# Sums of weight blocks in the gate and product buffers, and both seven-product fours of a chunk one behind the other

## What is computed

```python
D_FF = 5632
def swiglu(x, w_gate, w_up, w_down):
    return (jax.nn.silu(x @ w_gate) * (x @ w_up)) @ w_down

x = x + 0.5 * swiglu(rmsnorm(x, ffn1_norm[i]), ffn1_w_gate[i], ffn1_w_up[i], ffn1_w_down[i])
x = x + hybrid_mixer(...)
x = x + 0.5 * swiglu(rmsnorm(x, ffn2_norm[i]), ffn2_w_gate[i], ffn2_w_up[i], ffn2_w_down[i])
```

## Time and profile before

| | us |
|---|---|
| median of 3 runs | 2666.16 (2665.12 to 2667.31) |
| the profiled execution | 2666.6 |
| its span, first to last instruction | 2664.8 |
| PE busy | 2597.6 (97%) |
| VectorE busy | 1769.4 (66%) |
| ScalarE busy | 1259.4 (47%) |
| GpSimd busy | 202.7 (8%) |

### The profile page before, as it was taken

How to read it: one execution, slowest core, us unless ns; L and a number is a source line. 1 busy time by engine, 2 the same in 40 slices (tenths; PEclk the granted TensorE clock), 3 DMA queues, 4 the chain that set the end, 5 groups by cost and what they waited for, 6 DMA issues and landing times.

```text
span 2664.8 us, 32709 instructions
## 1 busy us (share of the span) xinstructions
PE 2597.6 (97%) x11549; PEld 2132.5 (80%) x11549; DVE 1769.4 (66%) x2077; ACT 1259.4 (47%) x1464; POOL 202.7 (8%) x345
## 2 busy tenths in 40 slices
PE   9999999999999999999999999999999899999998
PEld 8888888777777778888888888888877777778887
DVE  7766766887778765556555665555677787776554
ACT  5544554554444444444444554444454444444333
POOL 0121100000000000001100410000000000000000
PEclk9999999999999999999999999999999999999999
DMA  7887775565665676668765676666765556657554
GB/s 220 258 252 234 216 231 170 195 207 189 219 206 197 202 231 213 207 211 259 244 210 175 215 226 210 208 209 208 220 199 189 197 199 207 200 190 259 194 193 158
DMA packets 280067, 561.53 MB, mean 211 GB/s; under 512 B 22826, under 2 KB 25784, under 8 KB 279720
## 3 DMA queue, kind: packets, MB, share of 16 engines
q1 hardware_dynamic: 257120, 489.61, 56.4%
q0 software_dynamic: 22208, 70.19, 8.5%
q10 hardware_dynamic: 648, 0.52, 0.1%
HBM read 526.02 MB, written 34.22 MB: 210 GB/s over the span
## 4 chain that ended last, share of the span: by engine, by line
PE 54%; issue 22%; DMA 11%; DVE 9%; ACT 2%; POOL 1%; DVEq 0%; ACTq 0%; SPq 0%; POOLq 0%
PE acc L635 45%; DMA raw<-in_ffn_w_up 7%; DVE wlo L1637 6%; PE acc L747 2%; PE acc L754 2%; PE acc L750 2%; DMA raw<-in_ffn_w_gate 2%; ACT whi L1164 2%; DMA qk<-turn_dram 1%; DMA turn_dram<-turned_s 1%; DVE raw L1667 1%; PE s_ps L854 1%; DVE raw L1657 1%; PE tr L770 1%; DMA turn_dram<-mix_turned 1%
## 5 line engine op out<-in xcount | busy, mean ns | idle before, releaser
L1637 DVE TENSOR_TENSOR wlo<-raw,whi 128x1024 fp32r<-128x1024 f32 (+2 forms) x1009 | 1191.9, 1200 | 763.4 <-ACT whi L1164 756.2
L1164 ACT ACTIVATE whi<-raw 128x1024 fp32r<-128x1024 f32 (+2 forms) x1009 | 1037.4, 1038 | 1113.9 <-PE acc L635 641.2
L635 PE MATMUL acc<-whi,act_hi 128*128 128x512 f32 (+1 forms) x1280 | 348.5, 393 | 0.1
L635 PE MATMUL acc<-whi,act_lo 128*128 128x512 f32 (+1 forms) x1280 | 341.2, 388 | 0.0
L635 PE MATMUL acc<-wlo,act_hi 128*128 128x512 f32 (+1 forms) x1280 | 341.1, 388 | 0.0
L747 PE MATMUL acc<-whi,act_hi 128*128 128x512 f32 x1040 | 294.1, 395 | 44.4 <-ACT whi L1164 44.4
L754 PE MATMUL acc<-wlo,act_hi 128*128 128x512 f32 x1040 | 293.2, 395 | 3.3 <-DVE wlo L1637 3.2
L750 PE MATMUL acc<-whi,act_lo 128*128 128x512 f32 x1040 | 292.3, 394 | 0.0
L635 PEld LDWEIGHTS acc<-whi,act_lo 128*128 128x128 f32 x1280 | 239.2, 188 | 50.4 <-DVEq L1756 0.4
L635 PEld LDWEIGHTS acc<-wlo,act_hi 128*128 128x128 f32 x1280 | 239.3, 188 | 50.1 <-DVE wlo L1637 0.4
L747 PEld LDWEIGHTS acc<-whi,act_hi 128*128 128x128 f32 x1040 | 192.8, 188 | 99.3 <-ACT whi L1164 60.7
(11 more groups left out here) (331 smaller groups left out, 2131.4 us busy)
## 6 DMA issues: line engine op xcount, KB each, us to landing
raw<-in_w_in SPq DMA_DIRECT2D x280, 512.0 KB, 4.4
raw<-in_ffn_w_gate SPq DMA_DIRECT2D x176, 512.0 KB, 5.2
raw<-in_ffn_w_up SPq DMA_DIRECT2D x176, 512.0 KB, 4.6
raw<-in_ffn_w_down SPq DMA_DIRECT2D x176, 512.0 KB, 4.6
raw<-in_w_out SPq DMA_DIRECT2D x64, 512.0 KB, 4.8
turn_dram<-h_turned POOLq DMA_DIRECT2D x25, 512.0 KB, 2.9
h_back<-turn_dram POOLq DMA_DIRECT2D x100, 128.0 KB, 2.9
raw<-in_w_sg_out SPq DMA_DIRECT2D x24, 512.0 KB, 4.2
```

What stands on the lines that cost most here:

```text
L635: return nc.tensor.matmul(pair[:, half, 0:width], left[:, j * TILES + t, half * P:(half + 1) * P], right[:, (first_group + j) % RING, t, 0 ...
L1164: nc.scalar.activation(whi[:, slot, tiles, 0:width], raw[:, slot, tiles, 0:width], ACT.Copy).then_inc(hi_ready, 1)
L1637: nc.vector.tensor_tensor(wlo[:, slot, tiles, 0:width], raw[:, slot, tiles, 0:width], whi[:, slot, tiles, 0:width].bitcast(F32), ALU.subtr ...
```

## The change

The block sums are written to `g_sb` (outer) and `h_sb` (inner) in place of `raw`, and ScalarE and VectorE split those two groups from there. They announce themselves on a semaphore `sums_made` in place of `raw_in`. A place of `raw` now belongs to the n-th load (`load_index`), not to the n-th group, so all four places hold loads: 16 loads in a chunk of 20 groups. The load n waits for the split of the group that load n - 4 belongs to (`place_of_load`). The order of a chunk is now: 0 to 3 left 2 to 5, 4 to 7 the first four, 8 to 11 the second four, 12 and 13 left 6 and 7, 14 to 19 right 2 to 7. `fours_out` moves with `LAST_FOUR` from position 13 to 11; the adding of the gate's bank becomes `left_out` and stands at `LEFT_DONE`, position 13; silu stays at position 15.

```diff
--- before.py
+++ after.py
@@ -105,17 +105,40 @@
     return [(part, k) for part in FOUR_PARTS]
-CHUNK_ORDER = ([("left", k) for k in range(2, 6)] + four(0) + [("left", 6), ("left", 7)] + four(1)
+CHUNK_ORDER = ([("left", k) for k in range(2, 6)] + four(0) + four(1) + [("left", 6), ("left", 7)]
                + [("right", k) for k in range(2, G_D)])
 CHUNK_GROUPS = len(CHUNK_ORDER)
 SUMS_PER_CHUNK = FOURS + 4 + 1
 LAST_FOUR = max(o for o, (kind, _) in enumerate(CHUNK_ORDER) if kind == "inner")
...
+LEFT_DONE = max(o for o, (kind, _) in enumerate(CHUNK_ORDER) if kind in ("left", "inner"))
 FFN_GROUPS = 2 * G_D + (FF_CHUNKS - 1) * CHUNK_GROUPS + CHUNKS * KF // TILES
 MIXER_GROUPS = 15 * G_D + CHUNKS * (2 * G_D + 2 + 6) + CHUNKS * G_D
 FFN_AT = [FIRST_GROUPS + CHUNKS * G_D]
 FFN_AT.append(FFN_AT[0] + FFN_GROUPS + MIXER_GROUPS)
 ALL_GROUPS = FFN_AT[1] + FFN_GROUPS
-KIND = {at + 2 * G_D + o: kind for at in FFN_AT for o, (kind, _) in enumerate(CHUNK_ORDER)}
+FOUR_AT = [o for o, (kind, _) in enumerate(CHUNK_ORDER) if kind == "four_left"]
+LOOPS = [at + 2 * G_D for at in FFN_AT]
+KIND = {at + o: kind for at in LOOPS for o, (kind, _) in enumerate(CHUNK_ORDER)}
+CHUNK_LOADS = sum(kind not in ("outer", "inner") for kind, _ in CHUNK_ORDER)
+def load_index(m):
+    n = m
+    for at in LOOPS:
+        if m >= at:
+            chunks, o = divmod(min(m - at, (FF_CHUNKS - 1) * CHUNK_GROUPS), CHUNK_GROUPS)
+            n -= chunks * (CHUNK_GROUPS - CHUNK_LOADS)
+            n -= sum(kind in ("outer", "inner") for kind, _ in CHUNK_ORDER[:o])
+    return n
+def place_of_load(n, below):
+    m = below - 1
+    while KIND.get(m) in ("outer", "inner") or load_index(m) != n:
+        m -= 1
+    return m
@@ -179,7 +202,7 @@
 def outer_tiles(m):
-    left, right = m % RING, (m + 1) % RING
+    left, right = load_index(m) % RING, load_index(m + 1) % RING
@@ -427,10 +451,12 @@
             at = Place()
             def load(w, k, col, width=W, extra=None):
-                slot = at.n["group"] % RING
-                if at.n["group"] >= RING:
-                    sp.wait_ge(lo_ready, at.target("group", 1 - RING))
+                n = load_index(at.n["group"])
+                slot = n % RING
+                if n >= RING:
+                    before = place_of_load(n - RING, at.n["group"])
+                    sp.wait_ge(lo_ready, at.target("group", before + 1 - at.n["group"]))
                 rows = w[k * TILES * P:(k + 1) * TILES * P, :].rearrange("(t p) n -> p t n", p=P)
                 main = width - (HEADS if extra is not None else 0)
                 cols = slice(col, col + main) if isinstance(col, int) else bass.ds(col, main)
@@ -1153,15 +1179,22 @@
                     return
                 width = LAT2 if LAT2_FIRST <= m < LAT2_END else W
                 slot = m % RING
-                target = raw_target(m)
-                if at.turn is not None:
-                    target = target + at.turn * (16 * at.adds["group"] // RING)
-                act.wait_ge(raw_in[slot], target)
+                if KIND.get(m) in ("outer", "inner"):
+                    at.n["made"] += 1
+                    act.wait_ge(sums_made, at.target("made"))
+                    source = g_sb if KIND[m] == "outer" else h_sb
+                else:
+                    place = load_index(m)
+                    target = raw_target(place)
+                    if at.turn is not None:
+                        target = target + at.turn * (16 * at.adds.get("load", at.adds["group"]) // RING)
+                    act.wait_ge(raw_in[place % RING], target)
+                    source = raw[:, place % RING, :, :]
                 if m >= RING:
                     act.wait_ge(group_used, at.target("group", n + 1 - RING))
                 tiles = slice(1, 2) if KIND.get(m) == "four_right" else slice(0, TILES)
-                nc.scalar.activation(whi[:, slot, tiles, 0:width], raw[:, slot, tiles, 0:width],
+                nc.scalar.activation(whi[:, slot, tiles, 0:width], source[:, tiles, 0:width],
                                      ACT.Copy).then_inc(hi_ready, 1)
             def groups(count, last_split=True):
@@ -1480,14 +1514,15 @@
                         act.wait_ge(four_summed, 1 if first_one else 2)
                         nc.scalar.activation(four_hi, four_raw, ACT.Copy).then_inc(four_rounded, 1)
                 at.n["turn"] = EX_FFN1 if first_one else EX_FFN2
-                for i in at.loop(act, FF_CHUNKS - 1, dict(group=CHUNK_GROUPS, unit=2, chunk=1, turn=1, paired=1)):
+                for i in at.loop(act, FF_CHUNKS - 1, dict(group=CHUNK_GROUPS, unit=2, chunk=1, turn=1, paired=1,
+                                                          load=CHUNK_LOADS, made=2 * FOURS)):
                     for j in paired():
                         if j == 5:
                             turned_hi(h_hi, i * 4, h_back[:])
                         if j == LAST_FOUR:
                             unit_ready()
                             nc.scalar.activation(g_sb[:, 0, :], q1[:], ACT.Copy).then_inc(q1_copied, 1)
-                        if j == LAST_FOUR + 2:
+                        if j == LEFT_DONE + 2:
                             act.wait_ge(acc_free[at.n["unit"] % 2], at.target("unit", 0, 2, 2) + 2)
                             for half in range(HALVES):
                                 last = nc.scalar.activation(g_sb[:, half, :], g_sb[:, half, :], ACT.Silu,
@@ -1634,7 +1669,7 @@
                     outer_sums(m + 1)
                 tiles = slice(1, 2) if KIND.get(m) == "four_right" else slice(0, TILES)
                 dve.wait_ge(hi_ready, at.target("group", n + 1))
-                nc.vector.tensor_tensor(wlo[:, slot, tiles, 0:width], raw[:, slot, tiles, 0:width],
+                nc.vector.tensor_tensor(wlo[:, slot, tiles, 0:width], split_source(m)[:, tiles, 0:width],
                                         whi[:, slot, tiles, 0:width].bitcast(F32), ALU.subtract).then_inc(lo_ready, 1)
                 if sums_next:
                     inner_sums(m + 1)
@@ -1643,32 +1678,38 @@
             def raw_filled(m):
-                target = raw_target(m)
+                n = load_index(m)
+                target = raw_target(n)
                 if at.turn is not None:
-                    target = target + at.turn * (16 * at.adds["group"] // RING)
-                dve.wait_ge(raw_in[m % RING], target)
+                    target = target + at.turn * (16 * at.adds.get("load", at.adds["group"]) // RING)
+                dve.wait_ge(raw_in[n % RING], target)
             def outer_sums(m):
                 raw_filled(m)
                 raw_filled(m + 1)
                 dve.wait_ge(lo_ready, at.target("group", m - 1 - at.n["group"]))
-                slot = (m + 2) % RING
-                nc.vector.tensor_tensor(raw[:, slot, :, :], raw_blocks[:, outer_tiles(m)[0], :],
-                                        raw[:, (m + 1) % RING, 0, :].unsqueeze(1).to_broadcast([P, TILES, W]),
-                                        ALU.add).then_inc(raw_in[slot], 16)
+                nc.vector.tensor_tensor(g_sb[:], raw_blocks[:, outer_tiles(m)[0], :],
+                                        raw[:, load_index(m + 1) % RING, 0, :].unsqueeze(1).to_broadcast([P, TILES, W]),
+                                        ALU.add).then_inc(sums_made, 1)
+                at.n["made"] += 1
             def inner_sums(m):
-                raw_filled(m + 2)
+                dve.wait_ge(turned, at.target("turn", at.n["turn"] in (EX_FFN1, EX_FFN2)))
+                dve.wait_ge(sums_made, at.target("made"))
                 dve.wait_ge(lo_ready, at.target("group", m - at.n["group"]))
-                slot = (m + 3) % RING
-                at.n["sums"] += 1
-                nc.vector.tensor_tensor(raw[:, slot, 0, :], raw[:, (m + 2) % RING, outer_tiles(m)[1], :],
-                                        raw[:, (m + 1) % RING, 1, :], ALU.add).then_inc(sum_step, 1)
-                dve.wait_ge(sum_step, at.target("sums"))
-                nc.vector.tensor_tensor(raw[:, slot, 1, :], raw[:, slot, 0, :], raw[:, m % RING, 1, :],
-                                        ALU.add).then_inc(raw_in[slot], 16)
+                sum_settled(nc.vector.tensor_tensor(h_sb[:, 0, :], g_sb[:, outer_tiles(m)[1], :],
+                                                    raw[:, load_index(m + 1) % RING, 1, :], ALU.add))
+                nc.vector.tensor_tensor(h_sb[:, 1, :], h_sb[:, 0, :], raw[:, load_index(m) % RING, 1, :],
+                                        ALU.add).then_inc(sums_made, 1)
+                at.n["made"] += 1
+            def split_source(m):
+                if KIND.get(m) in ("outer", "inner"):
+                    return g_sb if KIND[m] == "outer" else h_sb
+                return raw[:, load_index(m) % RING, :, :]
             def paired():
                 for j in range(CHUNK_GROUPS):
@@ -1712,6 +1754,10 @@
```

(11 more changed lines are left out.)

## The result

The changed kernel takes 2596.14 us (median of 4 runs, 2593.17 to 2597.23) against 2665.81 us before (2665.12 to 2667.31): a ratio of 0.9736, 95% interval 0.9719 to 0.9753, 69.7 us less. The forecast was 2620 with a range from 2602 to 2646.

What follows compares the result with a forecast made beforehand. PE bounds the kernel; only its stops in 20 feed-forward chunks can be won, 4.0 us each. With 1.7 us left a chunk, 20 x (4.0 - 1.7) = 46 us, so 2666 - 46 = 2620 us, range 2602 to 2646.

Steps and rivals of the forecast that it cites:

- What bounds the kernel: PE is nearly always busy; only its stops in feed-forward chunks can be won, 4.0 us each, 80 us in 20.
- The loss behind the fours: PE's stops in front of groups 8 and 14, about 2.4 us a chunk, go as four loads lead instead of two.
- Gating starts at 0.2 us: VectorE's gating starts 0.2 us behind a chunk's group 0, not 1.98, as its run behind the products is broken up.
- The walk: Step-by-step VectorE start times through both fours, from group 0's start, giving PE's stops at groups 8 to 10.
- S: Start of the second four's outer sums: 11.1 us, or group 9's load landing if later; 11.75 taken with a 5.1 us load.
- The formula for PE's loss: PE loses S + 5.1 - 16.55 at group 8 if positive, about 1.0 at group 9, plus restarts: 1.7 us a chunk.
- the lower end of the working: With group 9's load landing at 10.8 us, PE loses 0.7 + 0.3 = 1.0 us a chunk; time 2606 us.
- Rival 1: VectorE enters the fours as late as now, gating near 1.98 us: loss 2.8 to 3.8 us, 2642 to 2662 us; chance 0.25.
- rival 4: Loads limited by DMA engines, so the ring leads by no more and plain groups still wait: 2660 to 2667 us; chance 0.06.
- Rival 2: No load is late and VectorE's last splits overlap better: loss 1.0 us or less, 2600 to 2606 us; chance 0.10.
- Rival 3: Slower: second outer sums await group 9's load ahead of split 7, each microsecond stopping PE for one; 2686 us; chance 0.04.
- the rule of interleaving: Regimes with different busiest engines may do better interleaved; packed fours put 14.5 us of VectorE's work against 9.5 of PE's.

Runs made afterwards that it cites:

- The best version here: The changed kernel with the split of the turned activations at position 12 instead of 5: 2579.21 us, ratio 0.9665 to the kernel of before.
- The buffers alone: The changed kernel with the chunk order put back to that of before, sums still in g_sb and h_sb: 2589.39 us, ratio 0.9705.
- the order alone: The kernel of before with the packed order and the gate's bank added two groups behind the products, sums still in raw: 2713.03 us, ratio 1.0162.
- the products late: The changed kernel with the products taken out at position 13 again, in one run with the gate's bank: 2594.88 us, ratio 0.9731.
- the two kernels with a late load: The changed kernel with group 9's load waiting for the split of group 4, or of group 5, instead of 3: 2656.80 us and 2663.27 us.
- again: The changed kernel itself measured once more, as the mark for other runs on the same chip: 2597.11 us, ratio 0.9733.

## Why the prediction fell short, point by point

**What bounds the kernel: right.** Only PE's stops at the fours could be won, 80 us by the working. The size was a little low, though. The best version here wins 89 us (2668.03 - 2579.21) against the kernel of before on its chip: the second block's periods average 46.8 us, not the 46.2 of the first, from which the 4.0 us a chunk were taken. Over both blocks PE lost 4.3 us a chunk.

**The loss behind the fours goes: right**, and it isn't due to the order. The buffers alone do it; the order alone makes the kernel slower.

**Gating starts at 0.2 us: right, with a reason that wasn't needed.** It does start at 0.20. The prediction named the broken-up run of VectorE and the lead of the loads. With the products late it still starts at 0.20, so the broken-up run decides nothing here. In the kernel with the order alone the packed order and the broken-up run bring it without the lead.

**The walk: right.** Predicted and measured, in us from group 0's start: gating 0.2 and 0.20, outer sums 4.1 and 4.14, split 3 5.2 and 5.25, inner sums 6.6 and 6.56, split 4 8.0 and 7.90, split 6 9.7 and 9.64. Behind it S + 1.1 and S + 1.21, S + 2.4 and S + 2.54, S + 3.8 and S + 3.88, S + 5.0 and S + 5.02. The formula for PE's loss, S - 11.45 + 1.05, holds within 0.04 us in 30 of 36 periods of the two kernels with a late load. So the mechanism at the second four was right.

**S: the term that was mis-sized.** This is the step that failed. The prediction took S = 11.75, a load of group 9 that lasts 5.1 us, set between rows of 4.6 and 5.5. The load took 3.5 us in the chunk shown and 3.9 at most, and S was 10.96, VectorE's own time. By the walk's own formula that is 0.5 us at group 9 and nothing at group 8; measured 0.46 and one restart of 0.1 or 0.2, 0.6 in all, where 1.7 was written. Two things were added on the safe side and should not have been: 0.2 us for the checks of the second outer sums, and a restart for a second stop that didn't come. Even the lower end of the working, 1.0 us, was above what came, since it kept both.

**What makes up the 24 us.** Three parts, by the periods of the two traces. The stop of 0.63 us instead of 1.7 is 20 x 1.07 = 21 us. (With S = 10.96 and the rest of the sum as written, the loss is 10.96 - 11.45 + 1.05 + 0.3 = 0.86 us and the time 2603 us, just inside the range.) The 4.0 us a chunk were 4.3, which is 7 us more gain. The longer chunks of the changed kernel bring its average loss to 0.8 us, not 0.6, and take 4 us back. In all, 20 x (4.3 - 0.8) = 70 us, as measured.

**Contention was turned round.** Group 9's load leaves 1.2 us ahead of the exchange's copies (6.49 against 640.57 - 632.90 = 7.67), and it was priced as though they would slow it. They were the ones that were slowed. The page's rows of the copies to `h_back`, first in the changed kernel, then in the one that holds the load back until 9.75 us, behind the copies:

```profile
h_back<-turn_dram POOLq DMA_DIRECT2D x100, 128.0 KB, 3.9
```

```profile
h_back<-turn_dram POOLq DMA_DIRECT2D x100, 128.0 KB, 2.9
```

2.9 us is also what the page has for them before the change. The load fares the other way: 3.5 to 3.9 us ahead of the copies, 4.2 to 5.4 when it leaves at 9.15 behind them. So the one issued later was the longer one under way. (The page's median of all w_up loads, 4.6 before, is no measure of this: it is 4.1 here, 3.9 in `again`, which is the same kernel, and 4.5 with the products late.) ScalarE now waits for the copies:

```profile
604.78 1.16 ACT L1278 ACTIVATE h_hi<-h_back 128x512 f32 x2 [1.18 <-DMA h_back<-turn_dram]
```

In the changed kernel that wait is all but covered in most chunks, as group 8's split is only just done then. Nothing in the prediction had that wait; in the old order, and in the longer chunks here, it shows.

**The rivals.** Rival 1 (a late start) and rival 4 (the ring doesn't lead) did not come. Rival 2 did, 4 us below its lower end of 2600. Rival 3's mechanism is real, and the prediction's slope for it; it decides the order alone and the late loads, and here the load came in time. The prediction weighed against the packed order the rule of interleaving (the Trainium skill, Perfetto Trace Analysis, Optimization Strategy). The trace agrees with it by 7.7 us: the old order with the buffers is faster. Once nothing waits for the exchange, the difference is gone.

**The chances.** Faster, at 0.92, came. The case that came, "no load is late", had been given only 0.10, though VectorE's own time was worked out step by step and the load's was set between rows from other places.

## What to carry to other kernels

A sum or a temporary that occupies a place of a load ring costs the lead of a load, even where its own engine has time; buffers that are idle in that stretch are a better home. When a walk gives two candidates for a start (an engine's own time, and a landing), let the one that is computed be the forecast and the guessed one the rival, unless a row shows it later. And before an engine's instructions are moved out of a stop's way, look at what would be waited for next: the same kind of edit, turned activations later, brought 17.9 us in the changed kernel and nothing in the kernel of before, where a load stood behind it.

## What the runs showed of the hardware

A stop of PE can cost more than its idle time, because the granted clock can be lower behind it. Besides the 3.5 us stop above, the kernel of before shows it. PE stands idle for 1.98 us until 658.00; these windows lie ahead of that stop and behind it, with the granted clock behind POOL's number:

```profile
651.00:655.90 4.90, 4.90 (x23) 3.81 (x21) 3.05 (x4) 1.07 (x1) 0.85 (x2) 1.00 0.81 240
659.40:662.00 2.60, 2.60 (x8) 2.02 (x7) 2.36 (x4) 2.00 (x3) 0.00 (x0) 0.52 0.08 29
```

The clock is 0.52 in the second, and 1.00 again from 662.0. The twelve matmuls of that group start at 658.00 and those of the next at 662.44, 4.44 us where 2.72 is the usual. It doesn't follow every stop of that size: behind the 1.56 us of the earlier trace rows the clock stays at 1.00 (611.10 to 618.00), and so it does behind the changed kernel's longest, 1.81 us (2065.41 to 2071.0). So a part of what the kernel of before lost in some chunks was the slow clock, which the prediction had in its 4.0 us a chunk without naming it.

GpSimd made a pause in one and the same chunk in all eleven traces, the fourth of the loop in the second block: between its second and third copy of the exchange it stood 2.51 us, and nothing shown in the profile was waited for. Before:

```profile
2101.88 1.09 POOL L548 DMA_DIRECT2D h_back<-turn_dram  x2 [2.51 <-issue]
```

and after:

```profile
2057.99 1.09 POOL L574 DMA_DIRECT2D h_back<-turn_dram  x2 [2.51 <-issue]
```

In the kernel of before that chunk held PE's longest wait for a rounding, 4.6 us by the earlier trace rows. In the changed kernel it is this stop of group 9's first product, behind ScalarE's wait for the exchange:

```profile
2065.41 0.50 PE L773 MATMUL acc<-whi,h_hi 128*128 128x512 f32 x1 [1.81 <-ACT whi L1197]
```

What GpSimd does in that time the runs don't show. With the turned split at position 12 the pause is still there (its pairs of copies are issued at 2044.14 and 2047.75), and costs nothing: that chunk lasts 42.16 us like the others.
